# Third feed-forward block: input products in two halves of 64 contraction rows

## What is computed

```
h2 = rms_norm(x, norm2_pre[i])
gate, up = jnp.split(h2 @ w_gate_up[i], 2, axis=-1)    # 1024 -> 2 * 2816
ffn = (jax.nn.silu(gate) * up) @ w_down[i]             # 2816 -> 1024
x = x + rms_norm(ffn, norm2_post[i])
```

## Time and profile before

| | |
|---|---|
| Time, median of 3 runs | 1145.37 us (1144.81 to 1145.86) |
| Span of the profiled execution, first to last instruction | 1142.2 us |
| Median of the runs less that span | 3.1 us |
| TensorE busy | 1125.3 us, 99% of the span |
| VectorE / ScalarE / GpSimd busy | 789.0 / 548.2 / 168.5 us |
| 20 tiles of the third block, 967.31 to 1076.75 us for the last 19 | 5.76 us a tile |
| Output products of the third block | 1076.75 to about 1136.2 us |

### The profile page before, as it was taken

One profiled execution on the slowest core, in us unless ns is written; L12 is line 12 of the kernel. 1 busy time (PEld: TensorE's weight loads), 2 busy tenths in 40 slices (PEclk: granted clock), 3 DMA queues, 4 the chain that ended last, 5 costly groups with the idle time before them and its releaser, 6 DMA issues.

```text
span 1142.2 us, 19373 instructions
## 1 busy us (share of the span) xinstructions
PE 1125.3 (99%) x7697; PEld 1028.8 (90%) x7697; DVE 789.0 (69%) x1089; ACT 548.2 (48%) x775; POOL 168.5 (15%) x211
## 2 busy tenths in 40 slices
PE   7999999999999999999999999999999999999998
PEld 6997899899998789989999988998779879999986
DVE  7998898777765648857777656686778776344443
ACT  6765344444443557845343354645544445333332
POOL 0132101111111011001111101550000001111100
PEclk9999999999999999999999999999999999999999
DMA  8453241636666556345666664554350456666552
GB/s 244 161 161 111 93 167 39 176 113 183 181 182 232 199 135 163 112 111 152 183 182 186 217 244 134 185 184 147 111 148 21 164 161 158 182 181 180 192 200 74
DMA packets 218387, 181.34 MB, mean 159 GB/s; under 512 B 42705, under 2 KB 196798, under 8 KB 218318
## 3 DMA queue, kind: packets, MB, share of 16 engines
q1 hardware_dynamic: 215566, 171.36, 49.9%
q0 software_dynamic: 2032, 6.88, 1.8%
q10 hardware_dynamic: 720, 2.13, 0.5%
HBM read 177.73 MB, written 2.62 MB: 158 GB/s over the span
## 4 chain that ended last, share of the span: by engine, by line
PE 84%; DVE 9%; ACT 2%; DMA 2%; issue 2%; POOL 1%; SPq 0%; DVEq 0%; POOLq 0%; ACTq 0%
PE bank L272 23%; PE bank L274 22%; PE bank L273 22%; PE bank L1308 3%; DVE ring L386 2%; PE bank L1165 1%; PE bank L2602 1%; DVE arena L1661 1%; PE bank L344 1%; DVE stat L1659 1%; ACT arena L380 1%; DMA ring<-in_w_out 1%; PE bank L358 1%; PE bank L2615 1%; PE bank L2547 1%
## 5 line engine op out<-in xcount | busy, mean ns | idle before, releaser
L272 PE MATMUL bank<-arena,arena 128*128 128x256 f32 (+2 forms) x1868 | 594.1, 318 | 2.0 <-DVE ring L386 1.6
L386 DVE TENSOR_TENSOR ring<-ring,arena 128x2048 fp32r<-128x2048 f32 (+1 forms) x136 | 305.3, 2248 | 156.1 <-ACT arena L380 155.6
L380 ACT ACTIVATE arena<-ring 128x2048 fp32r<-128x2048 f32 (+1 forms) x143 | 269.2, 1884 | 290.6 <-DMA ring<-in_ffn_w_in 107.7
L272 PEld LDWEIGHTS bank<-arena,arena 128*128 128x128 f32 x1868 | 356.3, 191 | 27.7 <-DVE ring L386 3.1
L273 PE MATMUL bank<-arena,arena 128*128 128x256 f32 (+1 forms) x1308 | 373.8, 286 | 0.0
L274 PE MATMUL bank<-arena,ring 128*128 128x256 f32 x1220 | 345.6, 283 | 0.0
L273 PEld LDWEIGHTS bank<-arena,arena 128*128 128x128 f32 x1308 | 251.1, 192 | 1.1
L274 PE MATMUL bank<-arena,arena 128*128 128x512 f32 (+3 forms) x644 | 239.5, 372 | 0.0
L274 PEld LDWEIGHTS bank<-arena,ring 128*128 128x128 f32 x1220 | 234.3, 192 | 0.0
L273 PE MATMUL bank<-ring,arena 128*128 128x512 f32 (+2 forms) x560 | 216.4, 386 | 0.0
L274 PEld LDWEIGHTS bank<-arena,arena 128*128 128x128 f32 x644 | 121.3, 188 | 20.7
(11 more groups left out here) (346 smaller groups left out, 1370.0 us busy)
## 6 DMA issues: line engine op xcount, KB each, us to landing
ring<-in_ffn_w_in SPq DMA_DIRECT2D x80, 512.0 KB, 4.9
ring<-in_ffn_w_out SPq DMA_DIRECT2D x44, 512.0 KB, 4.5
ring<-in_w_gate_up SPq DMA_DIRECT2D x40, 512.0 KB, 4.9
ring<-in_w_in SPq DMA_DIRECT2D x18, 1024.0 KB, 4.9
ring<-in_a_w_rkv SPq DMA_DIRECT2D x12, 1024.0 KB, 5.4
ring<-in_w_down SPq DMA_DIRECT2D x22, 512.0 KB, 3.7
ring<-in_a_w_o SPq DMA_DIRECT2D x4, 1024.0 KB, 8.9
arena<-in_ffn_w_in SPq DMA_DIRECT2D x8, 512.0 KB, 4.5
```

The costliest lines, as they stand in the source:

```text
L272: nc.tensor.matmul(dst, stationary[0], moving[0], start=start, stop=False)
L380: nc.scalar.activation(buf(hi_of(n), 0, w, arena12), ring[:, r, 0:w], ACT.Copy).then_inc(hi_ready, 1)
L386: on.tensor_tensor(ring12[:, r, 0:w], ring[:, r, 0:w], buf(hi_of(n), 0, w, arena12).bitcast(F32), ALU.subtract).then_inc(split_ready, 1)
```

## The change

For the third block alone (f == 2) each of the 20 looped tiles is computed differently. Each 128-row matmul becomes two matmuls of 64 contraction rows: rows 0 to 63 (upper) add up in bank `seat(j)`, rows 64 to 127 (lower) in bank `seat(j) + 4`. Upper and lower alternate, matmul by matmul. ScalarE copies the lower gate and lower up out of their bank to SBUF; VectorE adds the upper halves to them from the other bank; then the activation reads SBUF instead of PSUM, and the last product reads two SBUF operands. TensorE waits for the lower copies of all 20 tiles before the output products, which use banks 4 to 7. The early tiles and the first two blocks stay as they are.

```diff
+        def product_by_rows(dst, stationary, moving, start, stop):
+            for left, right, first, final in ((0, 0, start, False), (0, 1, False, False), (1, 0, False, stop)):
+                upper, lower = (nc.tensor.matmul(out, stationary[left][rows_], moving[right][rows_], start=first, stop=final)
+                                for out, rows_ in zip(dst, (slice(0, N), slice(N, P))))
+            return upper, lower
...
+                if f == 2:
+                    for g in range(2):
+                        if isinstance(it, int) and it == j == 0 and g == 1:
+                            early_turn(1, 1)
+                        dst = [bank[seat(j) + b][:, g * T:(g + 1) * T] for b in (0, RING)]
+                        for k in range(DC):
+                            upper, lower = product_by_rows(dst, both(w, slice(None), k, g), both(h2, slice(None), k), k == 0, k == DC - 1)
+                    upper.then_inc(upper_rows, 1)
+                    lower.then_inc(slot_done, 1)
+                    return
...
             rounds(pe, tile)
+            if f == 2:
+                pe.wait_ge(lower_copied, COPIED0 + FC - EARLY)
...
                     act.wait_ge(slot_done, first + it * RING + (j + 1))
-                    nc.scalar.activation(gate_act[seat(j)], bank[seat(j)][:, 0:T], ACT.Silu).then_inc(act_done, 1)
+                    if seat_taken(it, j):
+                        act.wait_ge(ffn_done, f * FC + it * RING + (j + EARLY - RING + 1))
+                    nc.scalar.activation(conv_acc[seat(j)], bank[seat(j) + RING][:, 0:T], ACT.Copy)
+                    nc.scalar.activation(gated[seat(j)], bank[seat(j) + RING][:, T:2 * T], ACT.Copy).then_inc(lower_copied, 1)
+                    act.wait_ge(rows_added, it * RING + (j + 1 + ADDED0))
+                    nc.scalar.activation(gate_act[seat(j)], conv_acc[seat(j)], ACT.Silu).then_inc(act_done, 1)
...
+                else:
+                    dve.wait_ge(lower_copied, it * RING + (j + 1 + COPIED0))
+                    dve.wait_ge(upper_rows, it * RING + (j + 1 + UPPER0))
+                    nc.vector.tensor_tensor(conv, gate, conv, ALU.add)
+                    nc.vector.tensor_tensor(gated[seat(j)], up, gated[seat(j)], ALU.add).then_inc(rows_added, 1)
+                    split_dve(dve, first + AHEAD + j, it)
+                    dve.wait_ge(act_done, f * FC + it * RING + (j + EARLY + 1))
+                    dve.wait_ge(rows_added, it * RING + (j + 1 + ADDED0))
+                    nc.vector.tensor_tensor(gated[seat(j)], gate_act[seat(j)], gated[seat(j)], ALU.mult).then_inc(ffn_prod, 1)
+                    return
```

More of the change, by code:

```diff
@@ L1045, in build @@
         early_mm, early_evacuated = u1_mm, q_in
+        upper_rows, lower_copied, rows_added = s1_zeroed, state_ready, u1_ready
+        UPPER0, COPIED0, ADDED0 = 1, 2, 2
         EARLY_MM0, EARLY_OUT0 = (1, 7, 14), 2
```

## The result

| | before | after |
|---|---|---|
| Median of 10 runs, us | 1144.74 (1143.59 to 1145.86) | 1146.59 (1145.56 to 1149.28) |
| Ratio, 95% interval | | 1.0021 (1.0013 to 1.0029) |
| Span of the profiled execution, us | 1142.2 | 1143.7 |
| 19 tiles after the first | 109.44 | 109.44 |
| Last start ahead of the first tile to the last of that tile | 6.18 | 6.72 |

The account below looks back on a forecast made before the run. TensorE's own matmul stream bounds the kernel; 0 (pairs) + 0.6 (height changes) + 1.8 (wait) = 2.4 us on a 1142.2 us span, plus 3.1 us, gives 1147.8 us. Own range 1146.7 to 1149.3 us; wider range 1140 to 1161.

Parts of the forecast that it names:

- The price of a pair: In the looped tiles of the third block, two half-height matmuls take 120 ns like one tall one: 0, bounds -10.6 and +12.5 us.
- A: Rival for the looped tiles: the other half hides fp32r's 13 ns, -10.6 us, 1137.2 us; chance 0.17, whole or part.
- B: Rival for the looped tiles: the 13 ns is spent in something shared, twice a pair, +12.5 us, 1160.3 us; chance 0.10.
- C: Rival for the looped tiles: no overlap for fp32r, 48 more matmuls of 0.12 us a tile, 115 us, 1263 us; chance 0.08.
- 13 ns: What an fp32r matmul of 256 columns carries above its 107 ns of streaming at 2.4 GHz: 120 less 107.
- The 4 ns for a further matmul: The skill's cost on a packed group for each further tile; over 960 pairs 3.8 us, 1151.6 us in all; not adopted.
- Changes of height: TensorE switching between 128 and 64 rows around the first tile's transposes: 0.2 us each, three open, 0.6 us, bounds 0.3 and 0.9.
- The wait: Ahead of the output products TensorE stands until ScalarE has copied the last tile's lower halves: 1.8 us, 1.0 to 2.8.
- VectorE's low part: VectorE's low-part weight split around the last tile starts 1.4 us later, behind copies and additions, and costs nothing.
- D: Rival in the hardware loop: the longer body no longer fits, three jumps back each wait, say 2 us; 1153.8 us; chance 0.07.
- The 3.1 us between span and median: What the forecast added to the span of 1144.6 us, as the median stands above the span, to reach 1147.8 us.
- no change: Outcome for the whole kernel within some 0.2%, 2.3 us, too small to tell; chance 0.21 + 0.08 = 0.29.

## Why the prediction was right

- **The bound** was read rightly: TensorE's stream alone. Both added costs passed one to one to the end (stretches longer by 0.54 and 1.62 us, 6.02 us behind the last matmul in both), and the work added to ScalarE and VectorE was hidden (height and wait taken back: 0.9998).
- **The price of a pair**, term 0: measured 0 to the nanosecond. 19 tiles take 109.44 us in both kernels. The cheaper and the dearer pair (A, B) and the pair without overlap (C) are out: a half keeps all of its 13 ns, and nothing of it is shared or hidden. The 4 ns for a further matmul of the Trainium skill ("TensorE: Matmul & The Clock Gate", Part 3), an estimated 3.8 us, don't appear in the throughput.
- **Changes of height**, 0.6 us: measured 0.54 us for the three open ones. They went when matmuls were tall again.
- **The wait**, 1.8 us: measured 1.62 us (61.38 for 59.76 us). The mechanism was as told, ScalarE held by a split that waited for a DMA. The term was 0.15 us too large: the DMA landed 0.1 us earlier against TensorE (the copies start 0.93 us after the last matmul's start, the activation before 1.04), and reaction and slow first distance together were 0.15 us, not 0.18. The two copies took 0.65 us for the 0.66 worked out. With ScalarE free at the end of the last matmul the prediction had 1.0 us; the run with the copies ahead of the split has that case and cost 1.1 us (60.88 for 59.76).
- **VectorE's low part** came 1.1 us later against the last matmul's start (2.28 for 1.17 us), not 1.4: the copies ended earlier and the two additions took 0.67 us from the first's start to the next instruction, not 0.85. It cost nothing either way.
- **Instructions** (D): the changed kernel has 51 transfers on queue 8 for 48, and 768 instructions more in the program (eight tiles that stand in it, by 96), so 256 a transfer. Three of them fall into the loop's first pass (984 to 1007 us), without a stop of TensorE; the window 1003 to 1085 us, with all later passes, has none on queue 8:

```profile
q1 hardware_dynamic: 21957, 14.75, 60.3%
q14 instruction: 2, 0.02, 0.1%
```

  A body of twice the length is kept whole. Of what the Trainium skill says ("Advanced Engine Details and Errata", ISA Cache), 128 KB for TensorE fits this, and "Only 2 cache lines!" doesn't: at its 256 instructions a line the body of 768 is three lines.
- **The sum**: 0.54 + 1.62 = 2.2 us in the trace, 2.4 forecast, 1.9 between the medians (interval of the ratio: 1.5 to 3.3 us). The spans differ by 1.5 us because the stretch ahead of the third block, which the change does not touch, was 0.7 us shorter in the profiled execution of the changed kernel. The 3.1 us between span and median were not all "around the span": in the ten executions of the changed kernel the time stands 1.8 to 2.5 us above the execution's own span, mostly 1.9. The rest came from setting the median of all runs against the span of one. It did no harm, as the same 3.1 us stood on both sides of the comparison.
- **Weaker**: the chance of "no change" was nearly a third, as the forecast stood on the border, and so does the result; the interval runs from 0.13 to 0.29%, across the 0.2% taken as the limit. The median, 1146.59 us, lies 0.1 us below the forecast's own range of 1146.7 to 1149.3 us, since the kernel before came out at 1144.74 us for the 1145.37 that the sum started from; as a difference, the 1.9 us lie inside the 1.3 to 3.9 us that the range means. The terms themselves were not right by luck: the price was exact, the other two were a little too large, and none made up for another.

## What to carry to other kernels

Splitting a contraction that already fills the array buys nothing: price a matmul by its columns, and count what the split adds, here a bank that must be emptied before the next stage may use it. When two stages share banks, begin the second stage in the banks that came free first; here 12 matmuls of cover took the gap from 1.63 to 0.21 us. Where work really is only 64 or 32 rows high, alternate the halves closely: three of one before the other still overlapped in full here, twelve did not, and nothing between was run.

## What the hardware showed that was not expected

- Matmuls on different rows overtake one another, but only some three places deep: blocks of 3, 12 and 24 gave 5.76, 8.45 and 9.99 us a tile. With 12 and 24, each change of half saves 3.2 places; with 3, all three.
- Four streams of 32 rows kept 120 ns a matmul each in the undisturbed tiles (5.76 us for 192), a start every 30 ns on the mean, with a weight load for each.
- At that density instructions run for the first time came too late (five stops, 7.0 us in all), while a loop with 768 matmuls in its body ran from what was already there (no transfer on queue 8 from 1018 to 1085 us).
